# GpSimd folds the two halves of the sum of squares in the first and third RMS norm of a two-block fp32 kernel

## The reference

```python
h = rmsnorm(x, norm_mix_g)             # first norm of block 1 ("norm 0" of the kernel)
x = x + mix(h) @ w_o
h = rmsnorm(x, norm_ffn_g)             # norm 1
x = x + conv_ffn(h, w_up, ffn_conv_w, w_down)
x = rmsnorm(x, norm_final_g)           # norm 2, taken together with norm1_g_2 of block 2
x = x + second_mix(...) @ w_out_2
x = x + square(relu(rmsnorm(x, norm2_g_2) @ w_up_2)) @ w_down_2      # norm 3
```

## Time and profile before

| what | value |
|---|---|
| time before, median of 3 runs | 1117.82 us (1117.53 to 1117.89) |
| profiled execution: time | 1118.39 us |
| profiled execution: span of the instructions | 1116.6 us |
| TensorE busy | 1110.0 us, 99% |
| VectorE busy | 749.6 us, 67% |
| ScalarE busy | 588.2 us, 53% |
| GpSimd busy | 166.8 us, 15% |

### The profile page before, as it was taken

One profiled execution on the slowest core, in us unless ns is written; L12 is line 12 of the kernel. 1 busy time (PEld: TensorE's weight loads), 2 busy tenths in 40 slices (PEclk: granted clock), 3 DMA queues, 4 the chain that ended last, 5 costly groups with the idle time before them and its releaser, 6 DMA issues.

```text
span 1116.6 us, 22664 instructions
## 1 busy us (share of the span) xinstructions
PE 1110.0 (99%) x9999; PEld 1090.0 (98%) x9999; DVE 749.6 (67%) x855; ACT 588.2 (53%) x696; POOL 166.8 (15%) x108
## 2 busy tenths in 40 slices
PE   9999999999999999999999999999999999999998
PEld 8999999999999999999999999999889999999998
DVE  7888776344567996886779667555666556656452
ACT  7667443423755664555765434423896346444331
POOL 0001442001232000000557000000010012201000
PEclk9999999999999999999999999999999999999999
DMA  8445332234465555555465443445445555555552
GB/s 301 147 151 189 125 135 94 113 118 148 151 229 191 187 193 200 201 199 189 156 217 189 168 172 118 147 151 189 151 152 180 197 189 188 190 189 190 193 198 101
DMA packets 27601, 192.26 MB, mean 172 GB/s; under 512 B 3056, under 2 KB 3184, under 8 KB 4848
## 3 DMA queue, kind: packets, MB, share of 16 engines
q1 hardware_dynamic: 27504, 190.82, 48.9%
HBM read 189.76 MB, written 1.05 MB: 171 GB/s over the span
## 4 chain that ended last, share of the span: by engine, by line
PE 96%; ACT 1%; DVE 1%; issue 1%; POOL 1%; DMA 0%; ACTq 0%; DVEq 0%
PE psS L615 59%; PE psP L615 17%; PE psS L603 7%; PE psS L541 2%; PE psP L926 1%; PE psP L784 1%; PE psP L772 1%; PE psP L900 1%; PE psP L877 1%; PE psP L946 1%; PE psP L670 1%; PE psP L830 1%; ACT wh L974 1%; PE psP L839 0%; POOL ss L1778 0%
## 5 line engine op out<-in xcount | busy, mean ns | idle before, releaser
L1332 DVE TENSOR_TENSOR wl<-raw,wh 128x2048 fp32r<-128x2048 f32 (+1 forms) x178 | 417.4, 2347 | 118.8 <-ACT wh L974 117.6
L974 ACT ACTIVATE wh<-raw 128x2048 fp32r<-128x2048 f32 x176 | 337.1, 1916 | 250.0 <-DMA raw<-in_wts 249.8
L615 PE MATMUL psS<-Yh,wh 128*128 128x256 f32 x1040 | 295.5, 284 | 0.3 <-DVE Yl L1338 0.3
L615 PE MATMUL psS<-Yl,wh 128*128 128x256 f32 x1040 | 288.2, 277 | 0.0
L615 PE MATMUL psS<-Yh,wl 128*128 128x256 f32 x1040 | 288.1, 277 | 0.0
L615 PE MATMUL psS<-Xh,wh 128*128 128x256 f32 x848 | 239.3, 282 | 0.3 <-PE psS L615 0.3
L615 PE MATMUL psS<-Xl,wh 128*128 128x256 f32 x848 | 235.3, 278 | 0.0
L615 PE MATMUL psS<-Xh,wl 128*128 128x256 f32 x848 | 235.3, 277 | 0.0
L615 PEld LDWEIGHTS psS<-Yh,wh 128*128 128x128 f32 x1040 | 195.7, 188 | 3.1 <-issue 1.9
L615 PEld LDWEIGHTS psS<-Yl,wh 128*128 128x128 f32 x1040 | 195.8, 188 | 2.5 <-issue 1.9
L615 PEld LDWEIGHTS psS<-Yh,wl 128*128 128x128 f32 x1040 | 195.3, 188 | 0.0
(11 more groups left out here) (267 smaller groups left out, 1938.8 us busy)
## 6 DMA issues: line engine op xcount, KB each, us to landing
raw<-in_wts SPq DMA_DIRECT2D x176, 1024.0 KB, 4.8
raw<-in_wts SPq DMA_DIRECT2D x2, 512.0 KB, 6.1
gdn<-in_x SPq DMA_DIRECT2D x1, 1024.0 KB, 8.4
out<-head SPq DMA_DIRECT2D x4, 256.0 KB, 2.1
head<-in_x SPq DMA_DIRECT2D x1, 516.0 KB, 3.8
head<-in_x SPq DMA_DIRECT2D x1, 512.0 KB, 6.1
xf<-in_dr SPq DMA_DIRECT2D x1, 512.0 KB, 6.6
xf<-in_md SPq DMA_DIRECT2D x1, 384.0 KB, 6.2
```

Of the source, the lines that this page charges most:

```text
L615: mm = pe.matmul(bank[:, half], a[:, n % SLOTS, p, :], b[:, kk_, :], start=(first and i == 0), stop=(last and i == 2), skip_group_check=True)
L974: act.activation(wh[:, n % SLOTS], raw[:, n % SLOTS], ACT.Copy).then_inc(sem["wh"], 1)
L1332: return dve.tensor_tensor(out, a, b, op)
```

## The change

In norms 1 and 3 GpSimd, after the third addition of squares, waits for its own result (a new semaphore `ssf`) and adds the second half of `ss[0]` to the first, 128x256. Only this addition now raises `ss`, for which TensorE waits. TensorE makes one product of the ones with the first half instead of two. Norms 0 and 2 stay as they are.

```diff
@@ TensorE, norm(i)
                 else:
                     pe.wait_ge(sem["par"], 16)
+                if i in (1, 3):
+                    pe.matmul(psA[5][:, 0], ones, ss[0][:, 0], start=True, stop=True,
+                              skip_group_check=True).then_inc(sem["nsum"], 1)
+                    return
                 for g in range(2 if i == 2 else 1):
                     for half in range(2):
@@ GpSimd, add_squares(i, j)
                     src = (sq, t2)[g][j % 2][:]
-                    name = "ss" if j == 3 and i != 2 else "ssa"
+                    name = "ssf" if j == 3 and i != 2 else "ssa"
                     if j > 1:
                         pool.wait_ge(sem["ssa"], base + per * (j - 2) + g + 1)
                     tt(ss[g][:], ss[g][:], src, ALU.add, name)
+                if j == 3 and i != 2:
+                    pool.wait_ge(sem["ssf"], 1 if i == 1 else 2)
+                    tt(ss[0][:, 0], ss[0][:, 0], ss[0][:, 1], ALU.add, "ss")
```

More of the change, by code:

```diff
@@ L284 @@
 og ogh on onr or orh out pa_ par pb_ pc pe pn pt qd qk r1 r2 r3 raw0 raw1 raw2 raw3 rawh rb rd res4 rg ri rl ro row rr rs rsp rt rtT
-rtk rtp ry s0 sc sg silu sp sq sqh sqp sqr sr ss ss0 ssa st t0c tap tb tk tok tsa uw uwp vb nrw nrh nr r2c rb2 rh vn warm wh wh0 wl wl0 xq ws x0 x0h
+rtk rtp ry s0 sc sg silu sp sq sqh sqp sqr sr ss ss0 ssa ssf st t0c tap tb tk tok tsa uw uwp vb nrw nrh nr r2c rb2 rh vn warm wh wh0 wl wl0 xq ws x0 x0h
 x1 x1h x2 x3 x3h xT xTb xb xbh xres ya yah zp zs
```

## The result

The changed kernel is slower: 1122.79 us (median of 16 runs, 1119.73 to 1129.83) against 1120.51 us for the kernel before in the same series (16 runs, 1117.53 to 1122.07). The ratio is 1.0029, 95% interval 1.0018 to 1.0040, or +3.2 us (+2.0 to +4.5). Forecast were +1.9 us and a time of 1119.7. The ratio isn't that of the medians, which are 2.3 us apart (1.0020): three of the changed kernel's 16 runs took 1126.0 to 1129.8 us, and without these three the means are 1.9 us apart instead of 3.1. The same kernel measured twice more, with no run over 1123.8 us, gave 1.0020 (1.0008 to 1.0032) and 1.0018 (1.0009 to 1.0027), that is +2.2 and +2.0 us. The kernel before has a wider scatter than its first three runs showed: its 96 runs lie anywhere from 1117.4 to 1122.3.

A forecast was written before the change was run, and what follows sets the result against it. TensorE, busy 99% of the span, was taken to bound the kernel. Waits less the saved products gave 0.96 + 0.95 = +1.9 us, on 1117.82 us 1119.7 us; own range 1119.1 to 1120.6, wider range with rival A 1116.9 to 1121.0.

The forecast's parts named there:

- The mechanism of the wait: Norms 1 and 3: VectorE's second split keeps GpSimd's new addition out until 363.31; it ends at 363.90 and TensorE waits.
- Rival A: Norms 1 and 3: the addition isn't kept out, the sum is ready, only the gain remains: -0.86 us, 1116.96 us; 11%.
- rival B: VectorE's third split also goes ahead of the addition: 6.3 us in two norms, 1124.1 us; 6% with its one-norm half.
- Rival C: TensorE's wait also costs clock: half speed for 5 us after each wait, 5 us more, 1124.7 us; 2%.
- what was costed at nothing behind the norms: Third split, VectorE's `y`, `rb`, the third block and loads behind the norms shift within their slack, at no cost.
- a wait of 1.39 us. Less the 0.43 us product: Norm 1: TensorE's product starts 1.39 us late, less one product saved, 0.96 us net; norm 3 repeats it with 0.95.
- How the numbers follow: Whole kernel: 1117.82 + 1.9 = 1119.7 us, 0.17% slower, taking the run's own scatter as 0.2 us.
- The chances at 0.2%: Whole kernel, line at 1120.06 us: slower by over 0.2% 29 to 31%, within 67%, faster 2%.
- What else moves: Work behind the waiting product: nothing on TensorE can pass it, the others have slack; all costed at nothing.
- The gain: TensorE at norms 1 and 3: one product of 0.43 us fewer in each, hidden by nothing, -0.86 us in all.

The follow-up runs named there:

- after_again: The changed kernel run again with no edit; 1121.54 us, ratio 1.0020 to the kernel before.
- after_third: The changed kernel run a third time with no edit; 1120.79 us, ratio 1.0018 to the kernel before.
- wait_only: Changed kernel, but GpSimd folds into a scratch buffer and TensorE makes two products, still waiting for the fold; 1123.10 us, ratio 1.0039 to before.
- drop_only: Changed kernel without the fold, one product, leaving out half the sum of squares in norms 1 and 3; 1119.92 us, ratio 1.0004 to before.
- place10_drain: Changed kernel with the product at the eleventh tile, and third-block pauses of both stages made drains; median 1118.58 us, ratio 1.0018 to before.
- memset_wait: Two products as before; GpSimd writes zeros into a scratch buffer in place of the fold, and the norm waits for that; one run, 1117.6 us.
- place10: Changed kernel with the norm's product at the eleventh tile instead of the sixth; 1120.01 us, ratio 0.9998 to the kernel before.

## Why the prediction was wrong, step by step

**The mechanism of the wait stood, nearly to the hundredth.** The fold was kept out by the second split, got its turn ahead of the queued third, lasted 2.65 us (forecast 2.7) and ended 0.58 us after the split (0.59); the third split took 2.81 us ("about 2.8"); TensorE started 0.06 us behind it (0.08). Rival A, a fold that isn't kept out, is shown false by 2.65 us against 0.74 undisturbed, and rival B, a third split served first, by the row that ends at 366.79, while that split ends at 368.95. Rival C found nothing: the granted clock was 1.00 in the windows around both waits (364 to 374 and 950 to 956 us). And what was costed at nothing behind the norms did cost nothing: in `after_again` and `after_third` the distance to before stays the same to 0.01 us over the next 230 weight products.

**A term was left out of the sum.** I priced a norm at "a wait of 1.39 us. Less the 0.43 us product". The wait was 1.36. But behind a wait the product's two records start 321 ns apart instead of 215, so the product costs 0.11 us more than in a running stream. (From its start to that of the first weight product behind it are 0.35 us, 366.85 to 367.20; two products in a running stream have 0.67, 362.59 to 363.26, which less 0.43 leaves 0.24 for one.) So a norm is +1.03 us, not +0.96, and the two +2.06 us: 0.18%.

**What failed is the step "How the numbers follow".** It took "the run's own scatter" as 0.2 us, from three runs, and so took 1117.82 us as the kernel's time and 1121.0 as the end of the range. The three runs had happened to lie in the lowest group; 16 runs of the same kernel reach from 1117.53 to 1122.07 us, a scatter of 4.5 us. The changed kernel's median of 1122.79 stands on a before of 1120.51, not 1117.82: 1120.51 + 1.9 is 1122.4, already past the range. The chances at 0.2% suffered too, since the line of 1120.06 us was drawn 0.4 us above the forecast. That the scatter is made by the slow pitch, in stretches that come and go between executions of one program, is likely but not shown for the kernel before: both its traces are of short runs without such a stretch. "What else moves" also had no term for a slow pitch behind the product, which was 0.36 us at norm 3 of the first trace.

**The size of the ratio.** Steps of 2.06 us are 1.0018, at the lower end of the first interval (1.0018 to 1.0040) and within both later ones. The lowest runs agree: 1119.73, 1119.40 and 1119.67 us in the three series against 1117.53, 1117.36 and 1117.38, that is 2.0 to 2.3 us. The 1.1 us between that and +3.2 are about the weight of the three runs over 1125 us. None of these was traced, so what makes them long is open: the slow pitch behind a norm gives 0.36 us in the first trace and none in the other two, and slow stretches upstream gave up to 3.6 us in a trace. None of the 96 runs of before took over 1122.3 us, while `wait_only` (three of 11), `drop_only` (two of 12) and `place10_drain` (three of 12) have runs over 1124 us too, and the other versions none. Whether the change makes slow stretches or long runs more frequent was not settled.

**The gain was wrong in a way the sum hid.** "One product of 0.43 us goes from each of two norms. Nothing hides it" held behind a wait (`wait_only` against the changed kernel, 0.43 us). Without one, the stream behind the single product goes at the slow pitch, and only 0.07 us of 0.43 is left (`drop_only`). Had rival A come true, the time would have been about 1117.7 (1117.82 - 0.14, an estimate from these steps) and not 1116.96 us.

## What to carry to other kernels

A short operation on an idle engine isn't short where the operations of a busy engine keep it out (2.65 us here instead of 0.74): look at what the other engine runs at that very time, and take the price from a row of the same shape in the same company. Who waits for it decides the rest; here moving the consumer by five tiles, 1.7 us, took the loss away. At differences of a fifth of a percent, three runs don't give a kernel's time, and three long runs of 16 moved the ratio by about 0.1%: compare stage by stage in the traces, from an event that both share.

## What the hardware showed that was not expected

TensorE has two pitches for the same stream of 128x256 products at a granted clock of 1.00: 113.4 and 117.8 ns from start to start. Products of another kind in the stream, which stand between the weight products, switch between them. Behind two fp32 products in a running stream it was fast from the sixth weight product on (both norms of both traces of before and of `memset_wait`); behind one it was slow (six norms out of six in `drop_only`, `place10` and `place10_drain`) until one or two pause products, or the drain, had passed (in one of the six, norm 1 of `place10`, it was slow ahead of the product too); behind one with a pause product directly after it, fast within seven products (four of four). Behind a wait it was fast in five of six norms of the changed kernel and slow in the sixth, and with two products (`wait_only`) fast in one and slow in the other. What the two pitches are inside the engine no run here shows. 4% of pitch over 225 weight products is 1 us, more than the 0.86 us that the change was after.
